# Down products of six of eleven hidden tile pairs by a seven-product scheme in a hybrid decoder layer

## The reference

```python
def swiglu(x, wg, wu, wd):
    return (jax.nn.silu(x @ wg) * (x @ wu)) @ wd

def trunk_layer(x, attend, conv_prev, w_in_l, conv_w_l, w_out_l, wg_l, wu_l, wd_l, g_l, b_l):
    x = layer_norm(DN_ALPHA * x + 0.5 * swiglu(x, wg_l[0], wu_l[0], wd_l[0]), g_l[0], b_l[0])
    y, ks, vs, cs = token_mixer(x, attend, conv_prev, w_in_l, conv_w_l, w_out_l)
    x = layer_norm(DN_ALPHA * x + y, g_l[1], b_l[1])
    x = layer_norm(DN_ALPHA * x + 0.5 * swiglu(x, wg_l[1], wu_l[1], wd_l[1]), g_l[2], b_l[2])
    return x, ks, vs, cs
```

## Time and profile before

| | us |
|---|---|
| median of 3 runs | 1032.84 (1032.51 to 1033.01) |
| the profiled execution | 1032.17 |
| its span | 1030.4 |
| PE busy | 990.4 (96%) |
| PE weight loads busy | 967.2 (94%) |
| DVE busy | 687.4 (67%) |
| ACT busy | 466.8 (45%) |
| DMA | 108.19 MB, 105 GB/s |

### The profile page before, as it was taken

One profiled execution on the slowest core, in us unless ns is written; L12 is line 12 of the kernel. 1 busy time (PEld: TensorE's weight loads), 2 busy tenths in 40 slices (PEclk: granted clock), 3 DMA queues, 4 the chain that ended last, 5 costly groups with the idle time before them and its releaser, 6 DMA issues.

```text
span 1030.4 us, 18173 instructions
## 1 busy us (share of the span) xinstructions
PE 990.4 (96%) x7538; PEld 967.2 (94%) x7538; DVE 687.4 (67%) x984; ACT 466.8 (45%) x780; POOL 69.8 (7%) x80
## 2 busy tenths in 40 slices
PE   8979999999999999999999998979999999999994
PEld 8979999999999999999888998979999999999994
DVE  5788742577886468726667687988634587784456
ACT  4455531245445235546555456644521354553230
POOL 2000000000000000107142000000000000000004
PEclk9999999999999999999999999999999999999998
DMA  9255333123225344362022463042432222336402
GB/s 259 83 122 141 108 119 103 42 88 119 82 83 167 100 123 83 100 191 82 23 62 83 133 188 97 28 131 79 132 104 62 83 82 83 103 117 184 146 1 87
DMA packets 131594, 108.19 MB, mean 105 GB/s; under 512 B 13138, under 2 KB 129590, under 8 KB 131496
## 3 DMA queue, kind: packets, MB, share of 16 engines
q1 hardware_dynamic: 130368, 105.46, 34.5%
q10 hardware_dynamic: 1144, 1.57, 1.2%
HBM read 103.08 MB, written 4.95 MB: 105 GB/s over the span
## 4 chain that ended last, share of the span: by engine, by line
PE 71%; DVE 18%; ACT 6%; issue 4%; DMA 0%; DVEq 0%; POOL 0%; ACTq 0%; SPq 0%
PE banks L1057 26%; PE banks L1070 24%; PE banks L880 15%; DVE w_lo L1814 4%; DVE more_raw L1806 2%; DVE w_raw L1806 2%; ACT w_hi L1380 2%; DVE w_sum L1806 2%; PE banks L1242 1%; DVE w_lo L1783 1%; DVE ln_sq L1923 1%; DVE more_lo L1814 1%; ACT w_hi L1366 1%; ACT x_hi L1515 1%; PE banks L1288 1%
## 5 line engine op out<-in xcount | busy, mean ns | idle before, releaser
L1070 PE MATMUL banks<-h_hi,w_hi 128*128 128x280 f32 (+1 forms) x480 | 139.1, 290 | 0.0
L1070 PE MATMUL banks<-h_hi,w_lo 128*128 128x280 f32 (+1 forms) x480 | 139.0, 290 | 0.0
L1070 PE MATMUL banks<-h_lo,w_hi 128*128 128x280 f32 (+1 forms) x480 | 138.8, 289 | 0.0
L880 PE MATMUL banks<-x_hi,w_hi 128*128 128x280 f32 (+1 forms) x416 | 126.1, 303 | 2.9 <-DVE x_lo L2159 0.9
L1057 PE MATMUL banks<-x_hi,w_hi 128*128 128x280 f32 (+1 forms) x400 | 117.9, 295 | 10.6 <-ACT ln_sq L1471 8.7
L880 PE MATMUL banks<-x_lo,w_hi 128*128 128x280 f32 (+1 forms) x416 | 120.6, 290 | 0.0
L880 PE MATMUL banks<-x_hi,w_lo 128*128 128x280 f32 (+1 forms) x416 | 120.5, 290 | 0.0
L1057 PE MATMUL banks<-x_hi,w_lo 128*128 128x280 f32 (+1 forms) x400 | 116.9, 292 | 0.0
L1057 PE MATMUL banks<-x_lo,w_hi 128*128 128x280 f32 (+1 forms) x400 | 116.8, 292 | 0.0
L1783 DVE TENSOR_TENSOR w_lo<-w_raw,w_hi 128x1024 fp32r<-128x1024 f32 (+1 forms) x66 | 77.9, 1183 | 57.6 <-ACT w_hi L1366 57.2
L1057 PE MATMUL banks<-t_hi,w_hi 128*128 128x280 f32 x336 | 98.3, 293 | 0.7 <-issue 0.7
(11 more groups left out here) (238 smaller groups left out, 2654.4 us busy)
## 6 DMA issues: line engine op xcount, KB each, us to landing
w_raw<-in_ffn_w_down SPq DMA_DIRECT2D x30, 512.0 KB, 4.1
more_raw<-in_ffn_w_down SPq DMA_DIRECT2D x28, 512.0 KB, 3.8
w_raw<-in_ffn_w_gate SPq DMA_DIRECT2D x24, 512.0 KB, 4.0
w_raw<-in_ffn_w_up SPq DMA_DIRECT2D x24, 512.0 KB, 5.0
more_raw<-in_ffn_w_gate SPq DMA_DIRECT2D x20, 512.0 KB, 4.0
more_raw<-in_ffn_w_up SPq DMA_DIRECT2D x20, 512.0 KB, 5.1
w_raw<-in_w_in SPq DMA_DIRECT2D x14, 512.0 KB, 4.5
w_raw<-in_w_out SPq DMA_DIRECT2D x32, 128.0 KB, 2.9
```

The lines of the kernel that those rows point to most:

```text
L880: mm = nc.tensor.matmul(out[:, 0:n], w[:, t, :], x(k), start=(k == ends[0] and w is hi and x is rhs_hi), stop=(k == ends[1] and w is lo))
L1070: mm = nc.tensor.matmul(out, w[:, k - k0, c * P:(c + 1) * P], h[:, k, cols(half, f)], start=(k == 0 and w is hi and h is h_hi), stop=(ku = ...
```

## The change

The hidden tiles of pairs 0 to 5 are no longer multiplied plainly. Each pair of hidden tiles (2) with two halves of tokens (2) and four output tiles (a "quad", two by two) is again a 2 x 2 by 2 x 2 block product and is made with seven products for eight. For that DVE makes, in each of these pairs, four sums of the hidden blocks, in three operations: `hidden_combinations` 0 (two blocks, 560 columns), 1 and 2 (280 each, each on the one before), which ACT splits in one copy of 1120 columns (`hidden_combo_hi`) and DVE in one operation (`hidden_combo_lo`). Of h1 only one tile has still to be split by itself.

The order is now `GROUPS`: pairs 0 to 2; both quads for pairs 0 and 1 (and for tiles 0 and 1, plainly, as an eighth unit: `quad_first`); pairs 3 to 5; both quads for pairs 2 to 5; pairs 6 to 9; then a tail for the 8 tiles of pairs 6 to 9 with the old code. A quad has seven steps like a pair, of 12 matmuls in the first chunk (two pairs; weight blocks of 512 columns) and 24 in the second (blocks of 1024), with four block sums of its own; its products use the same banks by turns, and each is added by DVE to `x_res` straight from the banks (`quad_add`, 560 columns), signalled by the semaphores that the pairs use. There are 6 raw buffers for 8. The additions of the layer norm's bias to the residual for half 0 (f = 0) are moved on ACT from the end of `down` into the input projections.

```diff
-RAWS = 8
+RAWS = 6
 N_PAIRS = FT // 2 - 1
-A_PAIRS = 4
-A_TILES = 2 + 2 * A_PAIRS
-H_TILES = FT - A_TILES
-K_UNITS = (((0, 4), (4, 8), (8, A_TILES)), ((0, 4), (4, 8), (8, H_TILES)))
-KU = len(K_UNITS[0])
+S_PAIRS = ((0, 1), (2, 3, 4, 5))
+S_SLOT = (0, 1, 2, 0, 1, 3)
+N_SP = len(S_SLOT)
+C_FIRST = N_SP
+C_TILES = 2 * (N_PAIRS - C_FIRST)
+K_UNITS = ((0, 4), (4, C_TILES))
+KU = len(K_UNITS)
 C_PAIRS = KT // 2
+GROUPS = (("pair", 0), ("pair", 1), ("pair", 2), ("quad", 0, 0), ("quad", 0, 1), ("pair", 3), ("pair", 4), ("pair", 5),
+          ("quad", 1, 0), ("quad", 1, 1), ("pair", 6), ("pair", 7), ("pair", 8), ("pair", 9))
...
+        for key in GROUPS:
+            if key[0] == "pair":
+                out += [("st", f, key[1], s) for s in range(7)]
+            else:
+                out += [("sd", f, key[1], key[2], s) for s in range(7 if key[1] else 8)]
+        out += [("dn", f, 0, ku, None) for ku in range(KU)]
+        out += [("dn", f, cp, ku, half) for half in range(2) for cp in range(1, C_PAIRS) for ku in range(KU)]
...
+        rows_a = sb("rows_a", [P, 6, HALF])
+        silu_g, h_f32, ln_sum = rows_a[:, 0:2, :], rows_a[:, 2:4, :], rows_a[:, 4:6, :]
...
+        hs_hi = sb("hs_hi", [P, 4, 7, HALF], F32R, ffn_h)
+        sums_h = ExitStack()
+        hs_sum = sb("hs_sum", [P, 4, 7, HALF], F32, sums_h)
+        sums_h.close()
+        hs_lo = sb("hs_lo", [P, 4, 7, HALF], F32R, ffn_h)
...
+        def group_banks(G):
+            x = 2 * (G % 2)
             return banks[:, x:x + 2, 0:HALF], banks[:, 4:6, 0:HALF], banks[:, 6:8, 0:HALF]
...
+                        pe.wait_ge(h0_done, G - 1)
...
+                        pe.wait_ge(c11_done, G)
...
+                    pe.wait_ge(p1_copied, G + 1)
...
+            def quad_step(f, chunk, qd, s):
+                G, n, off = group(f, "quad", chunk, qd), quad_unit(f, chunk, qd) + s, N_META * f
+                x, y, z = group_banks(G)
+                js = S_PAIRS[chunk]
+                m, q = len(js), N_SP * f + js[-1] + 1
+                pe.wait_ge(lo_ready, n + 1)
+                group_free(f, G, s)
+                if qd == 0 and s in (2, 3, 4, 6):
+                    pe.wait_ge(h_combo_ready, q)
+                out, c0, e = ((x, 0, 0), (z, off, 1), (x, 0, 5), (y, 0, 3), (x, 0, 4), (y, 0, 2), (x, off, 6))[s]
+                hi, lo = split_hi(n, QT), split_lo(n, QT)
+                new = s in (0, 1, 3)
+                for k, j in enumerate(js):
+                    if qd == 0 and s in (0, 1):
+                        pe.wait_ge(h0_ready, N_PAIRS * f + j + 1)
+                    if qd == 0 and s == 5:
+                        pe.wait_ge(h1_ready, N_PAIRS * f + j + 1)
+                    for ab in range(2):
+                        for w, h in ((hi, hs_hi), (hi, hs_lo), (lo, hs_hi)):
+                            mm = nc.tensor.matmul(out[:, ab, c0:HALF], w[:, k, ab * P:(ab + 1) * P], h[:, S_SLOT[j], e, c0:HALF],
+                                                  start=(new and k == 0 and w is hi and h is hs_hi),
+                                                  stop=(k == m - 1 and w is lo), skip_group_check=not new)
+                mm.then_inc(steps_done, 1)
+            def quad_first(f, qd):
+                G, n, off = group(f, "quad", 0, qd), quad_unit(f, 0, qd) + 7, N_META * f
+                x, y, z = group_banks(G)
+                hi, lo = split_hi(n, 2), split_lo(n, 2)
+                pe.wait_ge(lo_ready, n + 1)
+                pe.wait_ge(h_ready, 4 * f + 4)
+                for i, (out, c, half) in enumerate(((z, 0, 0), (y, 0, 1), (x, 2, 0), (z, 2, 1))):
+                    if i == 3:
+                        pe.wait_ge(z_evacuated, 2 * f + qd + 1)
+                    c0 = off if half == 0 else 0
+                    for ab in range(2):
+                        for k in range(2):
+                            for w, h in ((hi, g_hi), (hi, g_lo), (lo, g_hi)):
+                                mm = nc.tensor.matmul(out[:, ab, c0:HALF], w[:, k, (c + ab) * P:(c + ab + 1) * P],
+                                                      h[:, k, half * HALF + c0:(half + 1) * HALF],
+                                                      start=(i == 3 and k == 0 and w is hi and h is g_hi),
+                                                      stop=(k == 1 and w is lo), skip_group_check=i < 3)
+                    mm.then_inc(steps_done, 1)
...
+                        act.wait_ge(h_combined, 3 * (N_SP * f + min(j - 1, N_SP)))
                     nc.scalar.activation(h0_sb[q % 2][:, :, :], x, ACT.Copy).then_inc(p1_copied, 1)
                 elif s == 2:
                     if j:
                         act.wait_ge(h1_done, q)
+                        act.wait_ge(h1_ready, q)
+                        act.wait_ge(h_combined, 3 * (N_SP * f + min(j, N_SP)))
...
+            def hidden_combo_hi(f, j):
+                q = N_SP * f + j
+                act.wait_ge(h_combined, 3 * (q + 1))
+                nc.scalar.activation(hs_hi[:, S_SLOT[j], 3:7, :], hs_sum[:, S_SLOT[j], 3:7, :], ACT.Copy).then_inc(h_combo_hi, 1)
...
+                    act.wait_ge(h0_done, G + 1)
+                    if j < N_SP:
+                        nc.scalar.activation(hs_hi[:, S_SLOT[j], 0:2, :], h0[:, :, :], ACT.Copy).then_inc(h0_hi_done, 1)
+                        hidden_combo_hi(f, j)
+                    else:
+                        nc.scalar.activation(h_hi[:, tail_tiles(j), off:HALF], h0[:, :, off:HALF], ACT.Copy).then_inc(h0_hi_done, 1)
...
+                if 4 <= m < 4 + 2 * KT:
+                    bias_residual((m - 4) // KT, [(m - 4) % KT])
...
+            def hidden_combinations(f, j, i):
+                q, h0 = N_PAIRS * f + j, 2 * ((N_PAIRS * f + j) % 2)
+                done = 3 * (N_SP * f + j)
+                t = hs_sum[:, S_SLOT[j], :, :]
+                if i == 0:
+                    dve.wait_ge(h1_done, q + 1)
+                    dve.wait_ge(h0_done, group(f, "pair", j) + 1)
+                    out, a, b = t[:, 3:5, :], rows_a[:, 4:6, :], rows_a[:, h0:5:4 - h0, :]
+                elif i == 1:
+                    dve.wait_ge(h_combined, done + 1)
+                    out, a, b = t[:, 5, :], rows_a[:, 5, :], t[:, 3, :]
+                else:
+                    dve.wait_ge(h_combined, done + 2)
+                    out, a, b = t[:, 6, :], rows_a[:, h0 + 1, :], t[:, 5, :]
+                nc.vector.tensor_tensor(out, a, b, ALU.subtract).then_inc(h_combined, 1)
+            def hidden_combo_lo(f, j):
+                dve.wait_ge(h_combo_hi, N_SP * f + j + 1)
+                i = S_SLOT[j]
+                nc.vector.tensor_tensor(hs_lo[:, i, 3:7, :], hs_sum[:, i, 3:7, :], hs_hi[:, i, 3:7, :].bitcast(F32), ALU.subtract
+                                        ).then_inc(h_combo_ready, 1)
...
+                if s == 0 and 0 < j <= N_SP and GROUPS[G % N_GROUPS - 1][0] == "pair":
+                    hidden_combo_lo(f, j - 1)
...
+                        hidden_combinations(f, j, 0)
+                        dve.wait_ge(h0_hi_done, q + 1)
+                        nc.vector.tensor_tensor(hs_lo[:, S_SLOT[j], 0:2, :], h0[:, :, :],
+                                                hs_hi[:, S_SLOT[j], 0:2, :].bitcast(F32), ALU.subtract).then_inc(h0_ready, 1)
+                        hidden_combinations(f, j, 1)
+                        hidden_combinations(f, j, 2)
...
+                elif s == 6 and j < N_SP:
+                    dve.wait_ge(h1_hi_done, q + 1)
+                    nc.vector.tensor_tensor(hs_lo[:, S_SLOT[j], 2, :], h1_sb[:, 1, :],
+                                            hs_hi[:, S_SLOT[j], 2, :].bitcast(F32), ALU.subtract).then_inc(h1_ready, 1)
+                    if GROUPS[G % N_GROUPS + 1][0] == "quad":
+                        hidden_combo_lo(f, j)
...
+            def quad_add(f, chunk, qd, block, bank, done, first=False):
+                r, half = block
+                c, off = 4 * qd + 2 * r, N_META * f if half == 0 else 0
+                x = x_res[:, c:c + 2, half * HALF + off:(half + 1) * HALF]
+                if first:
+                    op = nc.vector.scalar_tensor_tensor(x, x, ALPHA, bank[:, :, off:HALF], ALU.mult, ALU.add)
+                else:
+                    op = nc.vector.tensor_tensor(x, x, bank[:, :, off:HALF], ALU.add)
+                op.then_inc(done, 1)
...
+            def quad_step(f, chunk, qd, s):
+                G, n = group(f, "quad", chunk, qd), quad_unit(f, chunk, qd) + s
+                x, y, z = group_banks(G)
+                before = group(f, "quad", chunk - 1, qd) + 1 if chunk else 0
+                alone = chunk == 1
+                if s in (0, 2, 3, 4) or alone:
+                    dve.wait_ge(steps_done, FREE[n])
+                if s == 0:
+                    if alone:
+                        dve.wait_ge(z_evacuated, 2 * f + qd + 1)
+                    elif f:
+                        dve.wait_ge(res_biased, 4 * KT)
```

(36 more changed lines are left out.)

453 lines of the change are left out of this document (230 added, 223 removed).

## The result

| us | before | changed |
|---|---|---|
| median | 1033.01 (5 runs, 1032.51 to 1034.82) | 1093.86 (5 runs, 1088.65 to 1095.47) |
| the profiled execution | 1032.17 | 1088.65 |
| its span | 1030.4 | 1086.9 |

A forecast was written before the change was run, and what follows sets the result against it. Bound: PE, and in gate/up pairs a loop of PE, ACT and DVE with no slack. Sum: 1032.2 - 17.5 + 46.0 + 3.3 + 5.2 + 1.5 + 0.8 = 1071.5 us; range 1048 to 1086.

The forecast's parts named there:

- What bounds it, pairs, quads: Gate/up pairs and quads of both feed-forwards: added ACT and DVE work lengthens a loop without slack, +46.0 us.
- 1.6 and 1.8 in pairs 4 and 5: PE waits 1.6 us before step 2 for ACT's p1 copy, 1.8 before step 6 for the c22 add.
- 4.9 before step 2 of quad 0: First half of quad 0: PE waits 4.9 us for the residual add behind DVE's split of 1120 columns.
- 2.5 in its second half: Quad 0, second half, preparing pair 3's weights: DVE needs 7.1 us where PE has 4.6, a 2.5 us wait.
- 2.0 inside step 0 of quad 1: Quad 1 reads pair 5's h0 at once: PE waits 2.0 us for the h0 split.
- quad 1's 2.6 before step 2: Quad 1, first half: PE waits 2.6 us more before step 2.
- Layer norm and end: Feed-forward 0's norm can't follow the shortened half 1, +5.9 less 0.7 us; feed-forward 1's last outputs, +1.5 us.
- Clock: PE at its lower clock behind quad 0's stop, 1.2 us twice, and 0.9 at the layer norm: +3.3 (0 to 8).
- Raw buffers: Six buffers make only each feed-forward's second group of loads tight: +0.4 us each, +0.8 in all (0 to 10).
- Fewer matmuls: Both feed-forwards: 144 fewer matmuls on PE, -17.5 us if PE never waits longer.
- Rival (c): Late loads: 1 us in each of some 26 groups, 1097 us; chance 0.06.

The follow-up runs named there:

- the run with fillers: Changed kernel plus small matmuls that nothing reads, ahead of PE's waits at the stops in pairs and quads: 1083.91 us, ratio 1.049.

## Why the prediction was wrong

In the first point, stops are net of 0.13 again.

**What bounds it, pairs, quads:** right. The rows' arithmetic gave places and sizes: 1.6 and 1.8 in pairs 4 and 5 (1.5 to 1.7), 4.9 before step 2 of quad 0 (5.1), 2.5 in its second half (2.4), 2.0 inside step 0 of quad 1 (1.9). The 2.5 came out by luck: its 7.1 us are the sum of full durations, against the prediction's own rule of start to start, by which the same operations take 6.6, and they began 0.95 us later than it says (158.67 for 157.72), behind a weight split. Three things came out smaller: pair 1 of feed-forward 0 has no stop at p1, since PE itself was late; the second stop of a pair is short where the clock fell at the first; quad 1's 2.6 before step 2 is 1.0 to 1.2 for the same reason (2.5 to 2.7 where the clock held). Together 41.9 for 46.0; with the clock held, in the run with fillers, the stops outside pair 0 are 7 us longer than that. Moving the two instructions in pairs 0, 1, 3 and 4 gave 20.8 back, where this part had 19.8 for the pairs.

**Layer norm and end:** right, 5.4 for 5.2 and 2.3 for 1.5.

**Clock, the first step that failed:** "The 4.9 us stop at quad 0 is as long: 1.2 twice, and 0.9 at the layer norm below", +3.3, with bounds 0 to 8. Measured 16.5 in the trace; filling the stops gave 10 of it back in the medians, and 5.2 between profiled executions, the rest being waited away at the next stop. Two errors. A stretch costs 1.5 us rather than 1.2 where PE works through it, and 2.6 behind the stop at quad 0. And stops of 2.0 to 2.6 us (start to start) also brought the clock down, 5 of 8 of them in the changed kernel, while none of the eight of 1.6 to 1.8 us did. The prediction had a 0.35 us pause that costs nothing and a 4.4 us stop that does, and put every stop of 2 to 3 us with the first. The kernel before seemed to bear that out: its two stops of 2.8 us, before step 6 of pair 0, had no stretch at the lower clock behind them. TensorE: Matmul & The Clock Gate (HAM oscillation) in the Trainium skill warns of repeated idle gaps. The trace agrees, with 12 stretches at the lower clock ahead of the end for 3; the section is about longer gaps than these, so it gives no price for them. That such stops count should have been a rival with a price.

**Raw buffers, the second:** "A block takes up to 5.1 us from issue to landing", +0.8. Alone, in the kernel before, six buffers cost 8.7, and spreading the write gives 11 back in the changed kernel. The 5.1 is the page's median over the execution. "Only the second group of each feed-forward is tight" was right; that this group's loads meet the bias write was in the trace (23.7 us in that stretch) and wasn't looked up.

**Fewer matmuls:** 17.5 was the saving at full spacing. The matmuls of both feed-forwards at their ordinary distances take 14.7 us less, and PE starts on them 1.2 us later; why the distances are a little longer stays open.

**Rival (c)**, late loads at 1097, gave the nearest time by another mechanism: one group was late, not 26.

## What to carry over

A stop of PE can be paid twice, as time and as the lower clock behind it, so price a change by the length of each stop, not by their sum. The second price is due only where PE doesn't wait again right behind: of 16.3 us that the clock took here, 5 to 10 were real. Filling stops with work that nobody waits for tells the two prices apart. Where a loop over three engines has no slack, look for the idle stretch that a new operation fits into: the same two instructions cost 30 us in one place of the queues and next to nothing in another. Before buffers are given up, read how long the loads take in the stretch where they become tight, not the median of the profile's page.

## What the runs showed of the hardware

- A write of 1472.5 KB with 8 as its outermost dimension ran for 30 us at some 50 GB/s beside the loads, and made 512 KB blocks take 12 to 24 us; with 128 outermost it ran in under 12 us.
- In the slow case, from 68 to 80 us, the two queues move as many packets (381 and 389) and together keep 50.9% of the engines busy.
- The stop that this makes isn't repeatable: 7.5, 9.7, 10.7 and 15.6 us (rows of waits) in the profiled executions of four kernels with the same loads there.
- In the changed kernel all seven stops of 3.3 us or more, start to start, were followed by a stretch at the lower clock or had one begin in them; of those of 2.0 to 2.6 us five in eight; at 1.6 to 1.8 us none in eight. Over the 17 profiled executions none of 46 stops of 1.5 to 1.85 us did it, and three of 3.3 us, all before the same layer norm product, did not.
- A stretch at the lower clock costs 1.5 us where PE works through it, and nothing where the next wait takes it up (ratio 0.9992, 0.9982 to 1.0003, with two of them gone).
